# Head normalisation moved from VectorE to ScalarE, and the products of gathered keys with queries moved from VectorE to GpSimd

## What is computed

```python
def gathered_attention(q, kg, vg, valid):
    s = jnp.einsum('bthd,btkhd->bthk', q, kg) * (HEAD_DIM ** -0.5)
    s = jnp.where(valid[:, :, None, :], s, NEG)
    p = jax.nn.softmax(s, axis=-1)
    return jnp.einsum('bthk,btkhd->bthd', p, vg)

# sample tokens: 256 keys of 2049 are gathered out of a paged cache, through page_table
kg = jnp.where(is_past, ck[phys, off], k[bidx, nidx])
vg = jnp.where(is_past, cv[phys, off], v[bidx, nidx])

def mem_attention(qm, mk, mv):
    s = jnp.einsum('bthd,bmhd->bhtm', qm, mk) * (HEAD_DIM ** -0.5)
    p = jax.nn.softmax(s, axis=-1)
    return jnp.einsum('bhtm,bmhd->bthd', p, mv)
```

## Time and profile before

| | us |
|---|---|
| median of 3 runs | 657.33 (656.35 to 657.81) |
| the profiled execution, its own time | 656.87 |
| its span | 654.7 |

### The profile page before, as it was taken

The page is one execution under the profiler, slowest core; times in us unless marked ns, Lnnn a source line. Parts: engine busy times, 40 slices in busy tenths (PEclk is TensorE's granted clock), DMA queues, the critical chain, the costliest instruction groups (busy, mean ns, idle before and its releaser), DMA issues.

```text
span 654.7 us, 8625 instructions
## 1 busy us (share of the span) xinstructions
PE 574.6 (88%) x3514; PEld 362.4 (55%) x3514; DVE 297.1 (45%) x794; ACT 91.5 (14%) x215; POOL 42.8 (7%) x54
## 2 busy tenths in 40 slices
PE   6999999869999979999789996999999869778481
PEld 4556656556588757777566654875563424422130
DVE  1355675596765789788473386311001100100007
ACT  1001211014001232223100211011111101000010
POOL 0000000000100143223000000000000000000000
PEclk9999999995999989999899997799999979797896
DMA  8963044561244457564268645699999999999941
GB/s 301 374 247 128 2 162 187 184 195 49 67 128 132 125 182 235 139 218 140 88 257 343 231 209 226 239 394 407 419 366 419 420 419 419 421 418 420 420 189 68
DMA packets 47132, 163.51 MB, mean 250 GB/s; under 512 B 5842, under 2 KB 22700, under 8 KB 34420
## 3 DMA queue, kind: packets, MB, share of 16 engines
q1 hardware_dynamic: 38272, 138.78, 55.0%
q0 software_dynamic: 3472, 14.31, 6.4%
q10 hardware_dynamic: 5348, 9.86, 4.2%
HBM read 160.14 MB, written 2.77 MB: 249 GB/s over the span
## 4 chain that ended last, share of the span: by engine, by line
PE 65%; DVE 16%; DMA 15%; issue 2%; SPq 1%; ACT 0%; DVEq 0%
DMA ring<-in_w_up 13%; PE bank L665 12%; PE bank L494 10%; PE bank L939 6%; PE bank L456 4%; PE bank L926 4%; PE bank L784 4%; PE bank L908 4%; PE bank L1006 3%; PE bank L974 2%; PE bank L848 2%; PE bank L829 2%; PE bank L535 2%; PE bank L761 2%; DVE proj L1389 2%
## 5 line engine op out<-in xcount | busy, mean ns | idle before, releaser
L665 PE MATMUL bank<-work,ring 128*128 128x264 f32 x384 | 93.7, 397 | 0.0
L494 PE MATMUL bank<-ring,work 128*128 128x512 f32 (+2 forms) x224 | 90.5, 546 | 0.6 <-DMA ring<-in_w_in 0.6
L939 PE MATMUL bank<-ring,work 128*32 128x512 f32 x384 | 67.2, 672 | 19.6 <-DMA ring<-in_w_up 13.2
L665 PEld LDWEIGHTS bank<-work,ring 128*128 128x128 f32 x384 | 71.8, 193 | 16.0 <-issue 4.8
L494 PEld LDWEIGHTS bank<-ring,work 128*128 128x128 f32 x224 | 40.2, 190 | 31.0 <-issue 27.0
L2023 DVE SCALAR_TENSOR_TENSOR work<-work,bank 128x256 f32<-128x256 f32 x8 | 3.4, 422 | 100.9 <-ACT work L1276 100.9
L939 PEld LDWEIGHTS bank<-ring,work 128*32 128x32 f32 x384 | 18.4, 122 | 52.9 <-issue 52.8
L939 PE MATMUL bank<-proj,work 128*32 128x512 f32 x128 | 35.0, 697 | 10.4 <-DMA ring<-in_w_up 10.4
L926 PE MATMUL bank<-gates 128*128 128x256 f32 x144 | 36.6, 411 | 0.0
L2036 DVE COPY gates<-bank 128x512 f32<-128x512 f32 x8 | 5.5, 692 | 66.3 <-PE bank L1006 66.3
L926 PEld LDWEIGHTS bank<-gates 128*128 128x128 f32 x144 | 34.8, 335 | 0.5 <-issue 0.4
(11 more groups left out here) (305 smaller groups left out, 766.5 us busy)
## 6 DMA issues: line engine op xcount, KB each, us to landing
ring<-in_w_up SPq DMA_DIRECT2D x24, 2048.0 KB, 18.8
ring<-in_w_down SPq DMA_DIRECT2D x12, 2048.0 KB, 27.9
ring<-in_w_in SPq DMA_DIRECT2D x22, 1024.0 KB, 5.4
proj<-in_w_up SPq DMA_DIRECT2D x8, 2048.0 KB, 24.1
proj<-in_w_down SPq DMA_DIRECT2D x4, 2048.0 KB, 27.9
ring<-in_w_o SPq DMA_DIRECT2D x4, 1024.0 KB, 8.1
ring<-in_cache_mem_k ACTq DMA_DIRECT2D x1, 2048.0 KB, 7.8
ring<-in_cache_mem_v ACTq DMA_DIRECT2D x1, 2048.0 KB, 14.0
```

What stands on the lines that cost most here:

```text
L494: last = mm(bank[2 * (i % 2 if i < MEMC else 0) + t][:, 0:w], lhs[:, k, 128 * t:128 * t + 128], rhs[:, k % 4, :], start=(k == 0), stop=(k ...
L665: last = mm(b[:, 0:TOK], w[:, k, 128 * (n % 2):128 * (n % 2) + 128], xT[:, k, 0:TOK], start=(k == 0), stop=(k == KT - 1))
L939: last = mm(bank[5][32 * j:32 * j + 32, :], xTe[q // 2 % 2][:, k, s0:s0 + CAP], w2[j // 2][:, j % 2, r, :], start=(k == 0), stop=(k == KT ...
```

## The change

`normalise` is split. DVE keeps the reciprocal (`inverse(n)`), and ACT multiplies the two halves of P1. DVE takes `inverse(n + 1)` at the start of head n, ahead of `head_out`; before, it took `normalise(n)` there. ACT runs `normalise(n + 1)` behind the copy of P2, and `exps(n + 2)` now stands ahead of the gate tiles of head n. The 17 products of keys with queries go to POOL, two behind each pair of gathers of values but the first, and the rest behind the last pair. DVE keeps the 17 sums. The products use two buffers, `prod[0]` and `prod[1]`, so product i waits for sum i - 2.

```diff
@@ SP
                 if n == NU_WO:
-                    sp.wait_ge(kg_used, 1)
+                    sp.wait_ge(kd_mul, 17)
@@ ACT
+            def normalise(n):
+                act.wait_ge(at_r, n + 1)
+                st = 8 * (n % 3)
+                for t in range(2):
+                    s = P1[n % 3][:, 256 * t:256 * t + 256]
+                    last = act.activation(s, s, ACT.Copy, scale=stats[:, st + 4 + t:st + 5 + t])
+                last.then_inc(at_p, 1)
+
             exps(0)
+            normalise(0)
             exps(1)
             for n in range(NMH + H):
                 act.wait_ge(at_t, n + 1)
                 if n >= 2:
                     act.wait_ge(at_v, n - 1)
                 act.activation(P2[n % 2], bank[2 + n % 2][:, :], ACT.Copy).then_inc(at_pt, 1)
+                if n + 1 < NMH + H:
+                    normalise(n + 1)
                 if n == 0:
                     gate_out(11)
+                if n + 2 < NMH + H:
+                    exps(n + 2)
                 for g in HEAD_TILES[n]:
                     gate_out(g)
-                if n + 2 < NMH + H:
-                    exps(n + 2)
@@ POOL
-            for i in range(16):
-                if i % 2 == 0:
-                    pool.wait_ge(at_t, 3 + i // 2)
-                pool.indirect_dma_start(Vg[:, i, :], None, cv,
-                                        bass.IndirectOffsetOnAxis(ap=idx_sb[:, i:i + 1], axis=0)).then_inc(vg_in, 16)
+            def key_product(i):
+                if i == 0:
+                    pool.wait_ge(kg_in[0], 16 * 8)
+                    pool.wait_ge(kg_in[1], 16 * 8)
+                    pool.wait_ge(knew_in, 32)
+                    pool.wait_ge(qr_sb, 1)
+                if i >= 2:
+                    pool.wait_ge(kd_sum, i - 1)
+                pool.tensor_tensor(prod[i % 2], Kg[:, i, :] if i < 16 else knew, qrep, ALU.mult).then_inc(kd_mul, 1)
+
+            for i in range(8):
+                pool.wait_ge(at_t, 3 + i)
+                for k in range(2 * i, 2 * i + 2):
+                    pool.indirect_dma_start(Vg[:, k, :], None, cv,
+                                            bass.IndirectOffsetOnAxis(ap=idx_sb[:, k:k + 1], axis=0)).then_inc(vg_in, 16)
+                if i:
+                    key_product(2 * i - 2)
+                    key_product(2 * i - 1)
+            for i in (14, 15, 16):
+                key_product(i)
@@ DVE
+            def key_sum(i):
+                dve.wait_ge(kd_mul, i + 1)
+                link(V.tensor_reduce(ssc[:, H * i:H * i + H], heads_of(prod[i % 2]), AX.X, ALU.add), kd_sum)
+
-            def normalise(n):
+            def inverse(n):
                 dve.wait_ge(at_e, 2 * n + 2)
                 st = stats[:, 8 * (n % 3):8 * (n % 3) + 8]
-                link(V.reciprocal(st[:, 4:6], st[:, 2:4]))
-                s = P1[n % 3]
-                for t in range(2):
-                    link(V.tensor_scalar(s[:, 256 * t:256 * t + 256], s[:, 256 * t:256 * t + 256], st[:, 4 + t:5 + t],
-                                         None, ALU.mult), at_p if t else dchain)
+                link(V.reciprocal(st[:, 4:6], st[:, 2:4]), at_r)
...
             softmax(0)
+            inverse(0)
             softmax(1)
             kdots = 0
             for n in range(NMH + H):
-                normalise(n)
+                if n + 1 < NMH + H:
+                    inverse(n + 1)
                 if n >= 3 and n % 2 == 1:
                     head_out(n - 3)
...
-                        key_dot(kdots, H, qrep, Kg[:, kdots, :] if kdots < 16 else knew, prod[kdots % 2],
-                                kg_used if kdots == 16 else dchain)
+                        key_sum(kdots)
                         kdots += 1
```

More of the change, by code:

```diff
@@ L306, in layer @@
         proj_free, gate_ps, act_gate = sem("proj_free"), sem("gate_ps"), sem("act_gate")
-        st_ps, st_sb, qr_ps, kg_used, xr_ready = (sem(n) for n in ("st_ps", "st_sb", "qr_ps", "kg_used", "xr_ready"))
+        st_ps, st_sb, qr_ps, xr_ready = (sem(n) for n in ("st_ps", "st_sb", "qr_ps", "xr_ready"))
+        qr_sb = sem("qr_sb")
         rep_ps, rep_sb = sem("rep_ps"), sem("rep_sb")
@@ L314, in layer @@
         is_ps, is_act, is_dve = sem("is_ps"), sem("is_act"), sem("is_dve")
-        bias_ready = sem("bias_ready")
+        kd_mul, kd_sum = sem("kd_mul"), sem("kd_sum")
         at_s, at_m, at_e, at_p, at_t, at_pt, at_v, at_oe = (sem(n) for n in (
             "at_s", "at_m", "at_e", "at_p", "at_t", "at_pt", "at_v", "at_oe"))
+        at_r = sem("at_r")
         sa_d, sa_p, sa_a = sem("sa_d"), sem("sa_p"), sem("sa_a")
@@ L1653, in _ @@
             dve.wait_ge(qr_ps, 1)
-            link(V.tensor_copy(qrep, bank[2][:, :]))
+            link(V.tensor_copy(qrep, bank[2][:, :]), qr_sb)
             for k in range(KT):
@@ L1813, in _ @@
                         topk_round(i)
[L1814 to L1817, removed]
                 if n == 10:
```

## The result

| | before | changed |
|---|---|---|
| median, us | 657.37 (4 runs, 656.35 to 657.81) | 667.76 (4 runs, 666.06 to 669.70) |
| profiled execution, us | 656.87 | 666.85 |
| its span, us | 654.7 | 665.0 |

The ratio is 1.0168, 95% interval 1.0144 to 1.0191: slower by 10.4 us. The forecast was 673.5, in a range of 666 to 679. The first rival, "the reload is hidden", had given 667.6.

A forecast was written before the change was run, and what follows sets the result against it. PE, full in heads 1 to 9, was taken as the bound, so new waits count in full: -5.3 + 0.9, 15.5 us of waits and 5.1 for the clock make +16.2, giving 673.5 us, range 666 to 679.

The forecast's parts named there:

- the reload is hidden: Rival: POOL's library reload is hidden or costs no more than ScalarE's table load; +10.3 us, 667.6 us; chance 0.2.
- the late copy: DVE's values copy, behind waits for POOL's products and ACT's exponentials, ends 10.2 us after the turn's start, due at 7.0.
- The wait ahead of turn 11: PE's wait for DVE's multiplications disappears because ACT normalises earlier: 3.6 us and 1.7 of clock, -5.3 us.
- The three long waits: PE waits for DVE's copy ahead of values 4, 6 and 8: 3.2 us each, 2.4 at values 4 after the reload.
- the wait ahead of values 10: New PE wait for DVE's copy behind four merges and two sums: 0.9 us.
- the reload: GpSimd's library load ahead of the first product on POOL: 8 us, making PE wait 6.7 us ahead of turn 5.
- the bounds of 0.53 and 1.6: Price limits in us for one product on POOL: a same-size fill below, three streams one after another above; 1.15 taken.
- The clock: PE's lower granted clock after idle of more than some 2.6 us: 1.7 us, three times, 5.1 us.
- POOL becomes the bound: Rival: products on POOL cost 1.6 us, 677.1 us, or 2.0, 680.3; chance 0.15, shared with a reload above 11.
- the waits stay short: Rival: products of 0.55 us, copy waits of 2.0 each, clock stays up; 658.9 us, or about 663; chance 0.05.
- faster: Rival: only turn 11's gain remains, the copy coming within 7.0 us of the turn's start; -4.4 us, 652.9; chance 0.03.

The follow-up runs named there:

- both swaps: Changed kernel with DVE's copy ahead of the next head's reciprocal and POOL's products ahead of the gathers in each pair; 652.42 us, ratio 0.9916.
- copy first: Changed kernel with one swap on DVE: the copy of a pair's values ahead of the next head's reciprocal; 657.32 us, ratio 1.0011.
- products alone: Changed kernel with ScalarE's part undone: products on GpSimd, DVE normalises at the start of each head as before; 676.16 us, ratio 1.0294.
- products between the gathers: Changed kernel with the two products of a pair standing between its two gathers on POOL; 659.66 us, ratio 1.0049.
- product at the start: Changed kernel with a 128x128 fill and product on GpSimd ahead of its first transfer, each waited for; 670.82 us, one execution.

## Why the prediction came out as it did

**The mechanism of the late copy was right, step by step.** PE was full in heads 1 to 9 and took every new wait in full. The wait ahead of turn 11 went away as said. The three long waits stood where they were put, ahead of values 4, 6 and 8, at 3.0 us against 3.2; the wait ahead of values 10 was 1.3 against 0.9. The copy being held by DVE's wait for the exponentials, and these by POOL, is shown by three separate edits: move the copy (10.8 us of stage less), shorten POOL's part (13.9 less), or take the sums out from ahead of the softmax (14.5 less). All three leave the products on GpSimd and the multiplications on ScalarE, so the loss isn't the price of running them there, nor of GpSimd and DVE hindering each other: it is the price of what stands in line behind them. One name in the prediction is wrong: `values(10)` needs the copy of heads 8 and 9, not of 6 and 7. It is the copy that stands behind the four merges and two sums, so the estimate isn't touched.

**The step that failed is the reload**, taken as 8 us of POOL and "PE waits 6.7 us ahead of turn 5". It measured 0.07 us (twice 37 ns), and turn 5 did not wait. So the forecast of 673.5 was 5.7 us too high, and the measured 667.76 lies below the forecast's own range of 668.5 to 678; the whole range holds it because it was stretched over the rivals. The case with a reload inside the slack was among these, with a chance of 0.2 and a time of 667.6; it is what happened. That it fits to 0.2 us is in part luck, as the sum further down shows: its terms were off by up to 1.4 us, both ways.

No row before could price the reload; I took the build's instruction for a transfer that somebody waits for. The Trainium skill (GPSIMD Engine Reference, Instruction dispatch) says that the first call into freshly loaded code on GpSimd costs about 6 us. This trace doesn't show that cost: the first product started 0.10 us behind the gather ahead of it, and no product took longer than 1290 ns. The measurement decides.

**Mis-sized terms.** A product took 1.25 us in a row of two (records of 1276 ns) against 1.15; the bounds of 0.53 and 1.6 held. The reason given for 1.15, that a write can go beside a read "as in the fill", isn't in the fill's row, which names no input. So 1.15 was a choice between bounds. The estimate of 1.1 us from the figure of the Trainium skill (GPSIMD Engine Reference, Performance versus the Vector engine) is 0.15 low. The clock was taken as 1.7 us after each of three idle stretches. After the second and third it was 1.6 each (5.38 and 5.26 us for the gate tile instead of 3.83, and 0.1 to 0.2 for the scores); after the first it was 3.3: values 1.71 instead of 1.08, scores 2.07 instead of 1.13, gate tile 5.51 instead of 3.83. Table by windows of the changed kernel after the first wait:

```profile
285.90:290.00 4.10, 4.10 (x9) 2.22 (x10) 1.68 (x3) 0.76 (x2) 2.00 (x2) 0.53 0.25 66
290.00:295.00 5.00, 5.00 (x18) 3.94 (x18) 1.23 (x3) 1.09 (x4) 0.00 (x0) 0.70 0.00 0
```

The stage's sum with measured terms: three waits 9.0, their clock 6.5, values 10 at 1.3, turn 11 at -3.6 and its clock at -1.7, and 0.6 less ahead of the samples' maximum (0.94 to 0.35): +10.9, where the stage grew by 11.0 and the median by 10.4. The rival had 9.6, 5.1, 0.9, -5.3 and nothing for the last term: +10.3.

**The rivals.** "POOL becomes the bound" and "the waits stay short" didn't happen: products stayed at 1.25 us beside all of DVE's work, and 3.0 us of idle brought the clock down. The point that I gave for "faster", the copy within 7.0 us of the turn's start, proved to be the right one: the version with both swaps goes below it (the copy ends at 282.80, 5.9 us after turn 4 starts at 276.93), and is 5.5 us faster than before. It got there without a faster POOL, which the prediction had asked for: the copy no longer stands behind the exponentials, nor the products behind the gathers.

## What to carry to other kernels

When work leaves an engine that is not the bound, price the waits that its order takes on, not the time that it saves: an instruction that now waits for two other engines holds back each short instruction behind it, and here a 0.42 us copy behind such a wait cost 10 us, more than half of it by the clock of the engine that waited. Put what others wait for ahead of what itself waits. And where two candidates end within 0.2 us, read the releaser from the kernel's semaphores and test it with a swap; the profile's name was the wrong engine.

## What the runs showed of the hardware

- The build's reload of GpSimd's library became two records of 37 ns in the middle of the kernel, and of 11 ns at its start.
- A product of 128x512 float32 on GpSimd takes 1276 ns, one after another every 1.25 us, 1.8 times DVE's 0.69 us, and one of 128x128 takes 400 ns. It was the same beside DVE's sums and softmax as beside an idle DVE.
- The length of an idle stretch on TensorE didn't decide by itself whether the granted clock fell in this stage. After 1.61 to 1.63 us it stayed at 1.00 three times (copy first), after 1.35 and 1.36 us too (products alone). After 1.71 us it stayed twice, after 1.73 us it fell to 0.50 over 6.00 us (products between the gathers). In products alone it stayed at 1.00 after 2.48 and 2.47 us, and fell to 0.50 to 0.60 over the next 3.4 to 4.3 us after 2.47, 2.47 and 2.54 us, and to 0.67 after 2.16 us. At the first turn it fell after 2.40 us (0.67 over the next 5.16 us in the changed kernel), and after 2.64 us and more it fell every time. What such a fall cost was 1.6 to 1.7 us in most places, and 3.3 us at the first of three waits, ahead of values 4, in three kernels (changed, products between the gathers, product at the start).
